# Reordered stage behind an RWKV-7 recurrence, early operand splits, and layer norms whose variance is summed with tokens on partitions

## The chip, the core and the metric

The kernel runs on one core of one Trainium2 chip. Engines as the profile names them: PE is the TensorE matmul and PEld its weight load, DVE is VectorE, ACT is ScalarE, POOL is GpSimd, SP is the queue that issues most DMAs. The metric is device microseconds (us) of one launch; lower is better.

## The reference, cut to what matters

Two identical layers work on a residual stream of 1024 tokens by 1024 features. In each, one input projection feeds three head groups: sparse attention (o_a), an RWKV-7 recurrence (o_b) and a pooling mixer (o_c). The change touches what follows the recurrence, and every layer norm (five: one on the input, two in each layer).

```
# behind the recurrence: group norm of y over heads of 64, bonus, gate
ym = y.mean(-1, keepdims=True)
yv = jnp.square(y - ym).mean(-1, keepdims=True)
yn = ((y - ym) * lax.rsqrt(yv + GN_EPS)).reshape(B, S, RWKV_WIDTH) * lnx_g + lnx_b
bonus = (jnp.sum(r_h * k_h * r_k, -1, keepdims=True) * v_h).reshape(B, S, RWKV_WIDTH)
o_b = ((yn + bonus) * g)
mix = jnp.concatenate([rms_norm(o_a, attn_norm_g), o_b, o_c], axis=-1) @ w_out
x = layer_norm(ALPHA * x + mix, ln1_g, ln1_b)
ffn = jnp.square(jax.nn.relu(x @ mlp_w1)) @ mlp_w2
ple = jax.nn.sigmoid(x @ pe_gate + pe_gate_b) * (p @ pe_proj)
x = layer_norm(ALPHA * x + ffn + ple, ln2_g, ln2_b)
```

## The kernel before

Features lie on partitions and tokens along the free dimension, in eight feature tiles (`kt`, `mt`) and two token halves of 512 (`hf`). Each engine has its own program, written out by hand in order, and the engines wait for each other by semaphores; no scheduler changes the order. A layer is a long attention stage, eight tiles of the recurrence in a loop, the stage behind the recurrence, the output projection, layer norm 1, the gate projection with the embedding, eight MLP blocks in a loop, and layer norm 2. `meet` makes four engines wait for one another, since memory is reused across it.

**Dense products.** Output projection, gate and MLP multiply operands split into a high and a low part: three matmuls for each feature tile (L1087 to L1089), so 24 for one unit (one output tile, one token half). For the output projection, ScalarE copies the eight mixed tiles into `MH` (L1389), VectorE writes what is left over into `ML` (L1993), and the weights are split the same way into `WH` (ScalarE, L1385) and `WL` (GpSimd, L1590). All of it starts behind the meeting.

**The stage behind the recurrence** works on `LP`, three feature tiles with two heads each. TensorE sums each head (mean, L1069), VectorE centres (L1948), ScalarE squares into `G1` (the profile's `SH`, L1358) and scales r (`G3`, which is `KK`, L1359), GpSimd multiplies by k (L1582), TensorE sums the bonus (L1069) and the squares (L969: tokens become partitions, the moving operand has two columns), ScalarE takes the root (L1363), VectorE inverts (L1982), TensorE spreads the inverse over each head (L978), VectorE normalises (L1960), ScalarE applies gain and offset (L1368), VectorE adds the bonus (L1966) and multiplies by the gate (L1970). `post_seq` gives TensorE's order, and a step's PSUM bank is free once the step four places earlier was read. VectorE also scales the attention's output `A3` here (L1811).

**A layer norm.** TensorE spreads the mean over all partitions (L624), VectorE subtracts it (L1613), the squares come from ScalarE for half 0 (L1131) and from GpSimd for half 1 (L1433), two buffers each. TensorE sums the squares with a matrix of 1/1024, which gives the variance on all 128 partitions for 512 tokens (L629, 128x512). ScalarE takes the root (L1134), VectorE inverts it (L1620, 128x512) and multiplies (L1628 in layer norm 1, L1624 elsewhere). Then, for layer norm 1, VectorE applies gain and offset (L1631), ScalarE makes `XH` (L1141), VectorE `XL` (L1636); elsewhere ScalarE writes `X` (L1144). In the first layer norm VectorE computes an angle and ScalarE two sines in between. The finished `X` is stored by one DMA (L609).

Of the kernel before, what the change touches and what calls it, by code (L numbers as in the profile page):

```python
# [26 lines left out]
P = 128  # L27
# [17 lines left out]
FT = DFF // FB // P  # L45
ALPHA = (2 * DEPTH) ** 0.25
# [159 lines left out]
def trunk(nc, xT, pT, pos, w_in, w_uq, w_lr, w_pool, w_out, w_gate, w_pe, w_1, w_2, par, emb, con1, con2, out):  # L206
    cs_dram = nc.dram_tensor("cs_scratch", (2, P, S), F32, kind="Internal").ap()
    with ExitStack() as ctx:
# [107 lines left out]
        G1 = SH12[:, :, :]  # L316
        G4 = sb("G4", [P, 3, S], post)
# [7 lines left out]
        Y = sb("Y", [P, KT, S], m)  # L325
        WH = sb("WH", [P, 2, KT, P], m, F32R)
# [41 lines left out]
        LN_SUMS = 2 + 2 * FB  # L368
        ln_mu, ln_xc, ln_sq, ln_sqf, ln_var, ln_std, ln_xn, ln_out = (
# [93 lines left out]
        def feats(h):  # L463
# [3 lines left out]
        post_seq = [("mean", 0), ("mean", 1), ("mean", 2), ("bonus", 0), ("var", 0), ("bonus", 1), ("bonus", 2),  # L467
                    ("spread", 0), ("spread", 1), ("gate", 0), ("spread", 2), ("gate", 1), ("gate", 2)]
        by_vector = [("mean", 0), ("mean", 1), ("mean", 2), ("bonus", 0), ("bonus", 1), ("bonus", 2), ("spread", 0),
                     ("spread", 1), ("gate", 0), ("spread", 2), ("gate", 1), ("gate", 2)]  # L470
# [28 lines left out]
        m_high, m_low = sem("m_high"), sem("m_low")  # L499
        N_SPLIT = N_WOUT + KT + FB * N_F  # L500
# [42 lines left out]
        def _(e):  # L543
# [64 lines left out]
            e.wait_ge(ln_out, 16 * (1 + 2 * DEPTH))  # L608
            e.dma_start(out, X[:, :, :]).then_inc(out_stored, 16)  # L609
            e.wait_ge(out_stored, 16)  # L610
# [3 lines left out]
        def _(e):  # L614
            def layer_norm(u, landed=None, sums=None, total=None):

                for hf in range(2):
                    if landed:
                        e.wait_ge(landed[hf], 16)
                        for kt in range(KT):  # L620
                            mm = e.matmul(BK_[4 + hf], mean_ones, Y[:, kt, hs(hf)], start=kt == 0, stop=kt == KT - 1)
                    else:
                        e.wait_ge(ln_sum, sums + (hf + 1))
                        mm = e.matmul(BK_[4 + hf], mean_ones, total[:, hf, :], start=True, stop=True)  # L624
                    mm.then_inc(ln_mu, 1)
                for hf in range(2):
                    for kt in range(KT):
                        e.wait_ge((ln_sq, ln_sq_later)[hf], u * KT + (kt + 1))
                        e.matmul(BK_[6 + hf], mean_ones, SQ[:, 2 * hf + kt % 2, :], start=kt == 0, stop=kt == KT - 1)\  # L629
                         .then_inc(ln_sqf, 1)  # L630
# [341 lines left out]

            def head_spread(bank, values, i, hf):

                for t in range(NB // 2):
                    for g in range(2):
                        w = values[:, hf, i, t, g:g + 1].broadcast_to([P, HD])
                        mm = e.matmul(bank[HD * g:HD * (g + 1), t * P:(t + 1) * P], w, ident, start=True, stop=True)  # L978
                return mm

            with e.Fori(0, DEPTH) as L:
# [72 lines left out]
                for n, (what, i) in enumerate(post_seq):  # L1054
                    for hf in range(2):
                        if n >= 4:
                            post_read(e, L, post_seq[n - 4], hf)
                        if what == "var":
                            e.wait_ge(y_sq, L * 6 + (2 * (NP - 1) + hf + 1))
                            mm = head_sums(post_bank((what, i), hf), G1, hf)  # L1060
# [10 lines left out]
                post_read(e, L, ("gate", 0), 0)  # L1071
# [3 lines left out]
                def dense(n, i, ws, high, low, kts=KT, f=0, ready=None, halves=(0, 1)):  # L1075


                    e.wait_ge(w_low, L * N_SPLIT + f * N_F + (split_seq(i) + 1))
                    s = split_seq(i) % 2
                    for hf in halves:  # L1080
                        b = 2 * (n % 2) + hf
                        e.wait_ge(d_free[b], L * D_USES + f * (N_DENSE // 2) + (n // 2 + 1))
                        for kt in range(kts):
                            if ready:
                                ready(kt, hf)
                            w, q = ws(kt), hs(hf)
                            e.matmul(BK_[b], WH[:, s, w, :], high[:, kt, q], start=kt == 0, stop=False)  # L1087
                            e.matmul(BK_[b], WH[:, s, w, :], low[:, kt, q], start=False, stop=False)  # L1088
                            mm = e.matmul(BK_[b], WL[:, s, w, :], high[:, kt, q], start=False, stop=kt == kts - 1)  # L1089
                        mm.then_inc(d_full[b], 1)  # L1090

                for mt in range(KT):
                    dense(mt, ZW + mt, lambda kt: kt, MH, ML,
                          ready=(lambda kt, hf: e.wait_ge(m_low, L * KT + (kt + 1)) if hf == 0 else None)
                          if mt == 0 else None)
# [5 lines left out]
                for mt, hf in [(0, 0), (1, 0), (0, 1), (1, 1)] + [(mt, hf) for mt in range(2, KT) for hf in range(2)]:  # L1101
                    b = 2 * (mt % 2) + hf
                    if mt < 2:
                        e.wait_ge(ln_std, (L * 2 + 2) * 2)
# [19 lines left out]
        def _(e):  # L1124
            def layer_norm(u, gain=None, offset=None, dst=None, high=None, between=None):
# [6 lines left out]
                for hf in range(2):  # L1132
                    e.wait_ge(ln_sqf, u * 16 + KT * (hf + 1))
                    e.activation(STD[:, hf, :], BK_[6 + hf], ACT.Sqrt, bias=LN_EPS).then_inc(ln_std, 1)  # L1134
                if between:
                    between()
                for n in range(2 * KT):
# [96 lines left out]
            with e.Fori(0, DEPTH) as L:  # L1234
# [120 lines left out]
                for i in range(NP):  # L1355
                    for hf in range(2):
                        post_read(e, L, ("mean", i), hf)
                        e.activation(G1[:, i, hs(hf)], LP[:, i, hs(hf)], ACT.Square).then_inc(y_sq, 1)  # L1358
                    e.activation(G3[:, i, :], BZ[:, BR + i, :], ACT.Copy, scale=par_col("rk", i))\  # L1359
                     .then_inc(bonus_half, 1)  # L1360
                for hf in range(2):
                    post_written(e, L, ("var", 0), hf)
                    e.activation(G2[:, hf, :, :, :].rearrange("p i t g -> p (i t g)"),  # L1363
                                 post_bank(("var", 0), hf)[:, 0:3 * NB], ACT.Sqrt, bias=GN_EPS, scale=1.0 / HD)\
                     .then_inc(post_scalar, 1)
                for i in range(NP):
                    e.wait_ge(y_scaled, L * 3 + (i + 1))
                    e.activation(LP[:, i, :], LP[:, i, :], ACT.Identity, bias=par_col("lb", i),  # L1368
                                 scale=par_col("lg", i)).then_inc(y_affine, 1)
                meet(e, L, 2)  # L1370

# [14 lines left out]

                split_high(L, ZW)
                for kt in range(KT):
                    e.activation(MH[:, kt, :], mixed[kt], ACT.Copy).then_inc(m_high, 1)  # L1389
# [33 lines left out]
        def _(e):  # L1423
            def layer_norm(u):

                for kt in range(KT):
# [112 lines left out]
            with e.Fori(0, DEPTH) as L:  # L1539
# [39 lines left out]
                for i in range(NP):  # L1579
                    e.wait_ge(bonus_half, L * 3 + (i + 1))  # L1580
                    settle(e)
                    e.tensor_tensor(G3[:, i, :], G3[:, i, :], BZ[:, BK + i, :], ALU.mult).then_inc(bonus_in, 1)  # L1582
                meet(e, L, 2)

# [9 lines left out]
                for i in range(ZW, MLP0 - GAP):  # L1594
# [11 lines left out]
        def _(e):  # L1606
            def layer_norm(u, between=None, affine=None, high_before=0):
# [7 lines left out]
                if between:  # L1615
                    between()
                for hf in range(2):
                    q = hs(hf)
                    e.wait_ge(ln_std, u * 2 + (hf + 1))
                    e.reciprocal(RST[:, hf, :], STD[:, hf, :])  # L1620
                    e.drain()
                    if not affine:
                        for kt in range(KT):
                            e.tensor_tensor(Y[:, kt, q], Y[:, kt, q], RST[:, hf, :], ALU.mult).then_inc(ln_xn, 1)  # L1624
                    else:
                        for n in range(KT + 3):
                            if n < KT:
                                e.tensor_tensor(Y[:, n, q], Y[:, n, q], RST[:, hf, :], ALU.mult).then_inc(ln_xn, 1)  # L1628
# [173 lines left out]
            def inverse_rms(L):  # L1802
# [3 lines left out]
                e.reciprocal(RSD[:, :], RSD[:, :])  # L1806

            def scale_attention():

                for p in range(3):  # L1810
                    e.scalar_tensor_tensor(A3[:, p, :], A3[:, p, :], par_col("ag", p), RSD[:, :], ALU.mult, ALU.mult)  # L1811
# [23 lines left out]
            def rwkv_tile(T, more):  # L1835
# [28 lines left out]
            with e.Fori(0, DEPTH) as L:  # L1864
# [76 lines left out]
                with e.Fori(0, NB - 1) as t:  # L1941
                    rwkv_tile(L * NB + t, True)
                rwkv_tile(L * NB + (NB - 1), False)
# [28 lines left out]

                for i in range(NP):
# [17 lines left out]
                for kt in range(KT):  # L1991
                    e.wait_ge(m_high, L * KT + (kt + 1))
                    e.tensor_tensor(ML[:, kt, :], mixed[kt], MH[:, kt, :].bitcast(F32), ALU.subtract)\  # L1993
                     .then_inc(m_low, 1)
# [141 lines left out]
```

## Time and profile before

| | |
|---|---|
| time, median of 3 runs | 3576.71 us (3575.73 to 3585.78) |
| the profiled execution's own time | 3576.34 us |
| its span | 3574.3 us |
| PE, PEld, DVE busy | 3274.0, 2373.5, 1913.2 us |
| ACT, POOL busy | 1053.9, 1146.4 us |
| mean granted TensorE clock | 0.965 of full |

Busy time is counted as soon as an engine has an instruction in work. An fp32 matmul appears as two rows. The chain that ended last is followed back from the last instruction; the granted clock is the share of 2.4 GHz that TensorE was given in a stretch, 1.00 or 0.50 or a mix. Times within a layer are given for the first one; the second repeats them some 1751 us later.

### The profile page before, as it was taken

What the parts mean: (1) busy time and instruction counts of PE and PEld (TensorE: products, weight loads), DVE (VectorE), ACT (ScalarE), POOL (GpSimd) and SP (SyncE); (2) the same over time, 40 slices, a digit from 0 to 9 for tenths busy, and PEclk for the clock granted to TensorE, in tenths of its full rate; (3) what the DMA queues carried; (4) which work ended last, traced back from release to release, by engine and by line L of the source; (5) the groups of instructions that cost most, each with busy time, mean ns of one, the idle gap of its engine ahead of it and who ended that gap; (6) DMA issues with size and microseconds to landing.
All of it is one profiled execution on the core that took longest, in us unless ns stands there. A gap on an engine that the chain in (4) does not pass through costs nothing.

```text
span 3574.3 us, 61403 instructions
## 1 busy us (share of the span) xinstructions
PE 3274.0 (92%) x23080; PEld 2373.5 (66%) x23080; DVE 1913.2 (54%) x3061; ACT 1053.9 (29%) x1857; POOL 1146.4 (32%) x952
## 2 busy tenths in 40 slices
PE   7989967999999999999989998689899999999997
PEld 3444435876577888888735444368675788888884
DVE  5788996444623333333467899854526133333335
ACT  3333334442212211211235343344402111221212
POOL 1175632641212222222114755155222122222221
PEclk9999979999999999999999899799999999999998
DMA  3110000001111111111111001000011111111111
GB/s 123 45 33 21 29 23 6 0 1 36 48 36 48 47 47 47 53 47 48 40 55 33 28 24 33 11 6 0 7 31 58 42 51 49 47 47 47 48 46 47
DMA packets 43861, 132.72 MB, mean 37 GB/s; under 512 B 9280, under 2 KB 11840, under 8 KB 43072
## 3 DMA queue, kind: packets, MB, share of 16 engines
q1 hardware_dynamic: 37280, 122.41, 10.5%
q10 hardware_dynamic: 6432, 8.40, 0.9%
q8 instruction: 84, 1.38, 0.2%
q14 instruction: 65, 0.53, 0.0%
HBM read 117.15 MB, written 5.24 MB: 34 GB/s over the span
## 4 chain that ended last, share of the span: by engine, by line
PE 59%; DVE 14%; issue 10%; DVEq 10%; POOLq 2%; ACT 1%; POOL 1%; DMA 1%; PEldq 0%; ACTq 0%; SPq 0%; PEld 0%
DVE M L1715 8%; DVEq L1719 8%; PE wide L1087 7%; PE bank L1089 7%; PE bank L1087 7%; PE bank L1088 7%; PE wide L1089 7%; PE wide L1088 7%; PE wide L799 3%; DVE PB L1735 2%; PE wide L629 2%; PE bank L799 2%; POOLq L1591 1%; DVE WK L1717 1%; DVEq L1716 1%
## 5 line engine op out<-in xcount | busy, mean ns | idle before, releaser
L1590 POOL TENSOR_TENSOR WL<-WR,WH 128x1024 fp32r<-128x1024 f32 x160 | 403.1, 2519 | 1479.2 <-ACT WH L1385 1478.5
L669 PE MATMUL wide<-X,WR 128*128 128x512 f32 (+1 forms) x1088 | 504.7, 608 | 11.6 <-ACT X L1144 9.4
L1385 ACT ACTIVATE WH<-WR 128x1024 fp32r<-128x1024 f32 x160 | 168.2, 1053 | 735.6 <-PE bank L1089 430.2
L2019 DVE TENSOR_TENSOR RB<-RB 128x512 f32<-128x512 f32 x128 | 88.5, 692 | 549.0 <-ACT RB L1411 549.0
L669 PEld LDWEIGHTS wide<-X,WR 128*128 128x128 f32 x1088 | 202.7, 196 | 246.9 <-issue 220.9
L1715 DVE MAX8 M<-WK 128x8 f32<-128x512 f32 (+5 forms) x342 | 314.9, 921 | 23.7
L1717 DVE MATCH_REPLACE8 WK<-M,WK 128x512 f32<-128x512 f32 (+5 forms) x342 | 309.5, 905 | 1.2 <-issue 1.2
L1087 PE MATMUL wide<-XH,WH 128*128 128x512 f32 x640 | 261.6, 409 | 18.1 <-POOLq L1591 9.5
L1087 PE MATMUL bank<-XH,WH 128*128 128x512 f32 x640 | 255.7, 400 | 0.0
L1089 PE MATMUL wide<-XH,WL 128*128 128x512 f32 x640 | 252.8, 395 | 0.0
L1088 PE MATMUL wide<-XL,WH 128*128 128x512 f32 x640 | 252.5, 395 | 0.0
L1089 PE MATMUL bank<-XH,WL 128*128 128x512 f32 x640 | 249.2, 389 | 0.0
L1088 PE MATMUL bank<-XL,WH 128*128 128x512 f32 x640 | 249.0, 389 | 0.0
L1087 PE MATMUL wide<-HH,WH 128*128 128x512 f32 x512 | 201.3, 393 | 0.0
L1088 PE MATMUL wide<-HL,WH 128*128 128x512 f32 x512 | 199.4, 389 | 0.0
L1089 PE MATMUL wide<-HH,WL 128*128 128x512 f32 x512 | 199.4, 389 | 0.0
L1089 PE MATMUL bank<-HH,WL 128*128 128x512 f32 x512 | 199.2, 389 | 0.0
L1088 PE MATMUL bank<-HL,WH 128*128 128x512 f32 x512 | 199.2, 389 | 0.0
L1087 PE MATMUL bank<-HH,WH 128*128 128x512 f32 x512 | 199.2, 389 | 0.0
L2032 DVE TENSOR_TENSOR Y<-Y,bank 128x512 f32<-128x512 f32 x128 | 87.9, 687 | 171.1 <-PE bank L1089 171.1
L799 PE MATMUL wide<-SH 64*64 64x64 f32 x3840 | 153.2, 220 | 21.2 <-POOL SH L1525 14.6
L2032 DVE TENSOR_TENSOR Y<-Y,wide 128x512 f32<-128x512 f32 x128 | 88.0, 687 | 153.7 <-PE wide L1089 153.7
(318 smaller groups left out, 6399.2 us busy)
## 6 DMA issues: line engine op xcount, KB each, us to landing
WR<-in_w SPq DMA_DIRECT2D x128, 512.0 KB, 3.5
WR<-in_w_in SPq DMA_DIRECT2D x34, 512.0 KB, 3.5
WR<-in_w_out SPq DMA_DIRECT2D x16, 512.0 KB, 3.5
WR<-in_w_gate SPq DMA_DIRECT2D x16, 512.0 KB, 5.5
Y<-in_xT SPq DMA_DIRECT2D x2, 2048.0 KB, 13.3
out_T<-X SPq DMA_DIRECT2D x1, 4096.0 KB, 11.1
QZS<-QZ ACTq DMA_DIRECT2D x48, 64.0 KB, 2.0
QZS<-QZ ACTq DMA_DIRECT2D x64, 48.0 KB, 1.9
```

The lines of the kernel that those rows point to most:

```text
L669: mm = e.matmul(BK_[hf][:, 0:q.stop - q.start], WR[:, i % RING, kt, :], X[:, kt, q], start=kt == 0, stop=kt == KT - 1)
L799: mm = e.matmul(BK_[bank][chunk(c), j * CH:(j + 1) * CH], lhs[chunk(c), 2 * j + g, :], rhs[chunk(c), 2 * j + g, :], start=True, stop=True)
L1087: e.matmul(BK_[b], WH[:, s, w, :], high[:, kt, q], start=kt == 0, stop=False)
L1088: e.matmul(BK_[b], WH[:, s, w, :], low[:, kt, q], start=False, stop=False)
L1089: mm = e.matmul(BK_[b], WL[:, s, w, :], high[:, kt, q], start=False, stop=kt == kts - 1)
L1385: e.activation(WH[:, split_seq(i) % 2, :, :], WR[:, i % RING, :, :], ACT.Copy).then_inc(w_high, 1)
L1590: e.tensor_tensor(WL[:, s, :, :], WR[:, i % RING, :, :], WH[:, s, :, :].bitcast(F32), ALU.subtract)
L1715: e.max(M8[:, :], src)
L1717: e.match_replace(work, M8[:, :], src, DROPPED if drop else BIG)
L1719: e.drain()
L2019: e.tensor_tensor(RB[:, b, :], RB[:, b, :], RB[:, b, :], ALU.mult).then_inc(square_ready, 1)
L2032: e.tensor_tensor(Y[:, i, hs(hf)], Y[:, i, hs(hf)], BK_[b], ALU.add).then_inc(d_free[b], 1)
```

## The change

It has four parts.

1. Behind the recurrence, the squares are summed as each becomes ready, and the variance stands in front of the bonuses. Two of the eight operand tiles are split (high and low) and two more copied high, and the first weight block is split high and low, all ahead of the meeting; the first unit of the output projection takes the tiles in the order 6, 0, 1, 2, 3, 4, 5, 7. Paddings and the map `LOW_AT` place these operands where nothing live is overwritten.
2. The attention's output is scaled in the recurrence's loop, 128 tokens a tile.
3. A layer norm sums its squares with tokens on partitions: 4 matmuls with two moving columns for each tile instead of one with 512. Root and inverse are then taken of 128x8, and the inverse is spread back by 4 transposing matmuls per half (`spread_inverse`); VectorE multiplies straight from PSUM. GpSimd keeps four of its eight squares, ScalarE takes the others. In layer norm 2, ScalarE writes three tiles of X ahead of the second root.
4. The output is stored in four quarters as they are finished.

```diff
@@ sync @@
-            e.wait_ge(ln_out, 16 * (1 + 2 * DEPTH))
-            e.dma_start(out, X[:, :, :]).then_inc(out_stored, 16)
+            for n in range(KT // 2, 2 * KT + 1, KT // 2):
+                k, q = slice((n - 1) % KT // (KT // 2) * (KT // 2), (n - 1) % KT + 1), hs((n - 1) // KT)
+                e.wait_ge(ln_out, 16 * 2 * DEPTH + n)
+                e.dma_start(out[:, k, q], X[:, k, q]).then_inc(out_stored, 16)
@@ tensor: layer norm @@
-                        e.matmul(BK_[6 + hf], mean_ones, SQ[:, 2 * hf + kt % 2, :], start=kt == 0, stop=kt == KT - 1)\
-                         .then_inc(ln_sqf, 1)
+                        for t in range(LN_TOK):
+                            mm = e.matmul(BK_[6 + hf][:, 2 * t:2 * t + 2], SQ[:, 2 * hf + kt % 2, t * P:(t + 1) * P],
+                                          mean_ones[:, 0:2], start=kt + t == 0, stop=kt + t == KT + LN_TOK - 2)
+                        mm.then_inc(ln_sqf, 1)
+                        if (hf, kt) in ((1, 1), (1, KT - 1)):
+                            spread_inverse(u, int(kt > 1))
+            def spread_inverse(u, hf):
+                e.wait_ge(ln_inv, u * 2 + (hf + 1))
+                for t in range(LN_TOK):
+                    mm = e.matmul(BK_[6 + hf][:, t * P:(t + 1) * P],
+                                  STD[:, hf, 2 * t:2 * t + 1].broadcast_to([P, P]), ident, start=True, stop=True)
+                mm.then_inc(ln_spread, 1)
@@ tensor: behind the recurrence @@
-                post_read(e, L, ("gate", 0), 0)
+                post_read(e, L, ("spread", 2), 0)
                 keep_clock(2, 4)
                 meet(e, L, 2)
@@ scalar: layer norm @@
+                ahead = 3 if high is None and not between else 0
+                later_square(1)
+                deviation(0)
+                for kt in range(3, KT, 2):
+                    later_square(kt)
+                for n in range(ahead):
+                    write_out(n)
+                deviation(1)
+                if between:
+                    between()
+                for n in range(ahead, 2 * KT):
+                    write_out(n)
@@ scalar: behind the recurrence @@
+                split_mixed(L, 0, 2)
                 split_high(L, ZW)
                 ...
+                split_mixed(L, 2, M_EARLY)
                 ...
                 meet(e, L, 2)
+                split_mixed(L, M_EARLY, KT)
@@ gpsimd @@
-                for kt in range(KT):
+                for kt in range(0, KT, 2):
                 ...
+                split_low(ZW)
                 meet(e, L, 2)
@@ vector: layer norm @@
-                    e.reciprocal(RST[:, hf, :], STD[:, hf, :])
+                def invert(hf):
+                    e.wait_ge(ln_std, u * 2 + (hf + 1))
+                    e.reciprocal(STD[:, hf, 0:2 * LN_TOK], STD[:, hf, 0:2 * LN_TOK]).then_inc(ln_inv, 1)
                 ...
-                            e.tensor_tensor(Y[:, kt, q], Y[:, kt, q], RST[:, hf, :], ALU.mult).then_inc(ln_xn, 1)
+                            e.tensor_tensor(Y[:, kt, q], Y[:, kt, q], BK_[6 + hf], ALU.mult).then_inc(ln_xn, 1)
+                            if (hf, kt) == (0, KT - 3):
+                                invert(1)
@@ vector: recurrence and behind @@
+                scale_attention(t)
                 ...
-                bonus(0)
-                scale_attention()
-                for i in range(1, NP):
-                    bonus(i)
+                lows(0, M_AHEAD)
                 for hf in range(2):
                     post_read(e, L, ("var", 0), hf)
                 e.reciprocal(g2, g2).then_inc(y_rstd, 1)
+                bonus(0)
                 normalise(0)
                 normalise(1)
+                bonus(1)
                 gated(0)
                 normalise(2)
+                bonus(2)
                 gated(1)
                 gated(2)
                 meet(e, L, 2)
-                for kt in range(KT):
+                lows(M_AHEAD, KT)
```

VectorE behind the recurrence, before: `G` is the bonus, `A` the attention's output, and the RECIPROCAL the inverse of the root.

```order
L1954 TENSOR_TENSOR G<-wide,BZ 128x512
L1811 SCALAR_TENSOR_TENSOR A<-A,PAR,RSD 128x1024 x3
L482 REGISTER_ALU
L1954 TENSOR_TENSOR G<-bank,BZ 128x512
L482 REGISTER_ALU
L1954 TENSOR_TENSOR G<-bank,BZ 128x512
L482 REGISTER_ALU
L1954 TENSOR_TENSOR G<-wide,BZ 128x512
L482 REGISTER_ALU
L1954 TENSOR_TENSOR G<-wide,BZ 128x512
L487 REGISTER_ALU
L1982 RECIPROCAL G<-G 128x48
```

The same engine and place now, from the last centring on.

```order
L2033 SCALAR_TENSOR_TENSOR LP<-wide,LP 128x512
L2063 TENSOR_TENSOR ML<-PZ,MH 128x1024
L2063 TENSOR_TENSOR ML<-A,MH 128x1024
L495 REGISTER_ALU
L2072 RECIPROCAL G<-G 128x48
L490 REGISTER_ALU
L2039 TENSOR_TENSOR G<-wide,BZ 128x512
L490 REGISTER_ALU
L2039 TENSOR_TENSOR G<-wide,BZ 128x512
L490 REGISTER_ALU
L2045 TENSOR_TENSOR LP<-LP,bank 128x512
```

All bonuses have moved behind the inverse, the attention's scaling has left this place, and two low parts stand in front of the inverse.

ScalarE at the same place, before: `KK` is r scaled, `G` the root, `LP` gain and offset.

```order
L1359 ACTIVATE KK<-BZ,PAR 128x1024
L482 ISA
L1363 ACT_TABLE_LOAD
L1363 ACTIVATE G<-wide 128x24
L482 REGISTER_ALU
L1363 ACTIVATE G<-wide 128x24
L1367 ISA
L1368 ACTIVATE LP<-LP,PAR 128x1024
```

And now: `MH` is the high part of an operand tile, `WH` that of the weights.

```order
L1446 ACTIVATE KK<-BZ,PAR 128x1024 x2
L1439 ACTIVATE MH<-PZ 128x1024
L1438 ISA
L1439 ACTIVATE MH<-A 128x1024
L1420 ISA
L1431 ACTIVATE WH<-WR 128x1024
L490 ISA
L1452 ACT_TABLE_LOAD
L1452 ACTIVATE G<-wide 128x24
```

Three copies that stood behind the meeting stand in front of the root here; two more follow it.

TensorE in the first layer norm, before: the mean, then the sums of squares.

```order
L613 UNCONDITIONAL_BRANCH
L621 MATMUL wide<-Y,C 128x512 x16
L629 MATMUL wide<-SQ,C 128x512 x16
L981 UNCONDITIONAL_BRANCH
L981 ISA
```

Now (`STD` is the inverse root, spread by the identity in `C`).

```order
L624 UNCONDITIONAL_BRANCH
L632 MATMUL wide<-Y,C 128x512 x16
L646 MATMUL wide<-C,SQ 128x2 x40
L656 MATMUL wide<-C,STD 128x128 x4
L646 MATMUL wide<-C,SQ 128x2 x24
L656 MATMUL wide<-C,STD 128x128 x4
L1023 UNCONDITIONAL_BRANCH
```

Each of the 16 wide matmuls has become four narrow ones, and two groups of spreads stand among them: the first behind the second tile of half 1, the other at the end, ahead of the projection that follows.

## Rows read from the trace of the kernel before

**Rows 1.** Stretches: each engine's busy time (instructions), granted clock, DMA share, GB/s.

```profile
794.00:835.00 41.00, 33.54 (x188) 20.37 (x186) 27.76 (x32) 16.27 (x20) 9.34 (x4) 0.90 0.00 1
928.00:980.00 52.00, 44.73 (x121) 22.36 (x120) 48.90 (x69) 19.00 (x29) 11.68 (x9) 0.93 0.21 81
980.00:1780.00 800.00, 795.27 (x3439) 645.78 (x3437) 275.27 (x399) 155.12 (x213) 176.14 (x70) 1.00 0.14 46
```

**Rows 2.** The chain behind the recurrence: start, us, engine and line.

```profile
802.41 6.55 PE wide L969 x48
...
839.61 5.67 DVE ML L1993 x3
```

**Rows 3.** ScalarE behind the recurrence: start, us, instruction, idle before and releaser.

```profile
800.86 1.13 ACT L1359 ACTIVATE KK<-BZ,PAR 128x1024 f32<-128x1024 f32 x1
...
809.00 0.19 ACT L1363 ACTIVATE G<-wide 128x24 f32<-128x24 f32 x1 [3.79 <-PE wide L969]
...
830.58 1.06 ACT L1385 ACTIVATE WH<-WR 128x1024 fp32r<-128x1024 f32 x1 [4.96 <-PEq L522]
831.54 2.93 ACT L1389 ACTIVATE MH<-A 128x1024 fp32r<-128x1024 f32 x3
```

**Rows 4.** VectorE behind the recurrence, in order of time.

```profile
803.06 5.43 DVE L1811 SCALAR_TENSOR_TENSOR A<-A,PAR,RSD 128x1024 f32<-128x1024 f32 x3
...
815.18 0.44 DVE L1982 RECIPROCAL G<-G 128x48 f32<-128x48 f32 x1
816.90 0.69 DVE L1960 TENSOR_TENSOR LP<-LP,wide 128x512 f32<-128x512 f32 x1 [1.28 <-PE wide L978]
...
828.47 1.29 DVE L1970 TENSOR_TENSOR BZ<-wide,LP 128x512 f32<-128x512 f32 x2 [0.15 <-issue]
```

**Rows 5.** One line: ns min/median/max of a low part.

```profile
L1993 DVE TENSOR_TENSOR ML<-A,MH x6: 1210/1213/2535, 832.6 to 2587.1; 128x1024 fp32r<-128x1024 f32 x6
```

**Rows 6.** VectorE in a tile of the recurrence.

```profile
670.36 0.62 DVE L1847 TENSOR_TENSOR MT<-wide,MT 128x192 f32<-128x192 f32 x2 [4.80 <-PE wide L873]
```

**Rows 7.** Two stretches of 1 us within L969's two-column matmuls.

```profile
805.00:806.00 1.00, 1.00 (x11) 1.00 (x11) 1.00 (x1) 0.19 (x1) 0.01 (x1) 1.00 0.00 0
806.00:807.00 1.00, 1.00 (x7) 1.00 (x7) 1.00 (x2) 0.00 (x0) 0.00 (x0) 0.55 0.00 0
```

**Rows 8.** TensorE, 128 moving columns, 128-column weights: start, us.

```profile
1813.74 3.73 PE L656 MATMUL wide<-X,WR 128*128 128x128 f32 x32
```

**Rows 9.** Layer norm 1 of the first layer, in order of time, all engines.

```profile
948.18 0.60 ACT L1134 ACTIVATE STD<-wide 128x512 f32<-128x512 f32 x1 [9.11 <-PE wide L629]
...
959.59 0.69 DVE L1636 TENSOR_TENSOR XL<-Y,XH 128x512 fp32r<-128x512 f32 x1
960.37 3.35 DVE L1620 RECIPROCAL RST<-STD 128x512 f32<-128x512 f32 x1
...
977.60 1.48 DVE L1636 TENSOR_TENSOR XL<-Y,XH 128x512 fp32r<-128x512 f32 x2 [0.16 <-ACT XH L1141]
...
979.93 1.88 PE L1107 MATMUL wide<-PE_IN,PEW 128*128 128x512 f32 x4
```

**Rows 10.** Layer norm 2 of the first layer: TensorE's and ScalarE's first work behind it.

```profile
1803.98 9.92 PE L669 MATMUL wide<-X,WR 128*128 128x512 f32 x16 [4.07 <-ACT X L1144]
...
1816.30 1.28 ACT L1257 ACT_TABLE_LOAD   x1 [4.48 <-issue]
```

**Rows 11.** The first layer norm: VectorE's first inverse, ScalarE's second root.

```profile
44.08 3.35 DVE L1620 RECIPROCAL RST<-STD 128x512 f32<-128x512 f32 x1 [0.16 <-issue]
...
48.82 0.60 ACT L1134 ACTIVATE STD<-wide 128x512 f32<-128x512 f32 x1 [11.25 <-PE wide L629]
```

**Rows 12.** The last layer norm's writes, then DMA issues: KB each, median us to landing.

```profile
3551.44 11.38 ACT L1144 ACTIVATE X<-Y,PAR 128x512 f32<-128x512 f32 x16
...
out_T<-X SPq DMA_DIRECT2D x1, 4096.0 KB, 11.1
WR<-in_w SPq DMA_DIRECT2D x128, 512.0 KB, 3.5
```

More of the change, by code:

```diff
@@ L368, in trunk @@
         LN_SUMS = 2 + 2 * FB
+        ln_inv, ln_spread = sem("ln_inv"), sem("ln_spread")
+        LN_TOK = HALF // P
+        SQ_ACT = [kt % 2 for kt in range(KT)]
         ln_mu, ln_xc, ln_sq, ln_sqf, ln_var, ln_std, ln_xn, ln_out = (
@@ L464, in feats @@
             return slice(HD * (h % 2), HD * (h % 2) + HD)
[L467 to L470, printed above, removed]
+        post_seq = [("mean", 0), ("mean", 1), ("mean", 2), ("var", 0), ("bonus", 0), ("spread", 0), ("spread", 1),
+                    ("bonus", 1), ("gate", 0), ("spread", 2), ("bonus", 2), ("gate", 1), ("gate", 2)]
+        by_vector = [use for use in post_seq if use[0] != "var"]
         by_scalar = [("var", 0)]
@@ L971, in head_sums, with variances @@
                 return mm
+            def variances(L):
+                for i in range(NP):
+                    for hf in range(2):
+                        e.wait_ge(y_sq, L * 6 + (2 * i + hf + 1))
+                        bank = post_bank(("var", 0), hf)
+                        for t in range(NB // 2):
+                            c, q = (i * (NB // 2) + t) * 2, hf * HALF + t * P
+                            mm = e.matmul(bank[:, c:c + 2], G1[:, i, q:q + P], block_ones[:, 0:P:HD],
+                                          start=True, stop=True)
+                        if i == NP - 1 and hf == 0:
+                            mm.then_inc(post_full, 1)
+                return mm
             def head_spread(bank, values, i, hf):
@@ L1070, in _, with dense @@
                         mm.then_inc(post_full, 1)
-                post_read(e, L, ("gate", 0), 0)
+                post_read(e, L, ("spread", 2), 0)
                 keep_clock(2, 4)
                 meet(e, L, 2)
-                def dense(n, i, ws, high, low, kts=KT, f=0, ready=None, halves=(0, 1)):
+                def dense(n, i, ws, high, low, kts=KT, f=0, ready=None, halves=(0, 1), order=range(KT), low_at=range(KT)):
                     e.wait_ge(w_low, L * N_SPLIT + f * N_F + (split_seq(i) + 1))
@@ L1082, in dense @@
                         e.wait_ge(d_free[b], L * D_USES + f * (N_DENSE // 2) + (n // 2 + 1))
-                        for kt in range(kts):
+                        for k, kt in enumerate(order[:kts]):
                             if ready:
-                                ready(kt, hf)
+                                ready(k, hf)
                             w, q = ws(kt), hs(hf)
-                            e.matmul(BK_[b], WH[:, s, w, :], high[:, kt, q], start=kt == 0, stop=False)
-                            e.matmul(BK_[b], WH[:, s, w, :], low[:, kt, q], start=False, stop=False)
-                            mm = e.matmul(BK_[b], WL[:, s, w, :], high[:, kt, q], start=False, stop=kt == kts - 1)
+                            e.matmul(BK_[b], WH[:, s, w, :], high[:, kt, q], start=k == 0, stop=False)
+                            e.matmul(BK_[b], WH[:, s, w, :], low[:, low_at[kt], q], start=False, stop=False)
+                            mm = e.matmul(BK_[b], WL[:, s, w, :], high[:, kt, q], start=False, stop=k == kts - 1)
                         mm.then_inc(d_full[b], 1)
@@ L1131, in layer_norm, with later_square, deviation, write_out @@
                     e.activation(SQ[:, kt % 2, :], Y[:, kt, hs(0)], ACT.Square).then_inc(ln_sq, 1)
-                for hf in range(2):
+                def later_square(kt):
+                    e.wait_ge(ln_xc, u * 16 + (KT + kt + 1))
+                    if kt >= 2:
+                        e.wait_ge(ln_sqf, u * 16 + (KT + kt - 1))
+                    e.activation(SQ[:, 2 + kt % 2, :], Y[:, kt, hs(1)], ACT.Square).then_inc(ln_sq, 1)
+                def deviation(hf):
                     e.wait_ge(ln_sqf, u * 16 + KT * (hf + 1))
[L1134 to L1137, printed above, removed]
+                    e.activation(STD[:, hf, 0:2 * LN_TOK], BK_[6 + hf][:, 0:2 * LN_TOK], ACT.Sqrt, bias=LN_EPS)\
+                     .then_inc(ln_std, 1)
+                def write_out(n):
                     hf, kt = n // KT, n % KT
@@ L1592, in split_low @@
                     e.drain().then_inc(w_used, 1 + GAP * (i == MLP0 - GAP - 1))
-                for i in range(ZW, MLP0 - GAP):
+                for i in range(NP):
+                    e.wait_ge(bonus_half, L * 3 + (i + 1))
+                    settle(e)
+                    e.tensor_tensor(G3[:, i, :], G3[:, i, :], BZ[:, BK + i, :], ALU.mult).then_inc(bonus_in, 1)
+                split_low(ZW)
+                meet(e, L, 2)
+                for i in range(ZW + 1, MLP0 - GAP):
                     split_low(i)
```

103 lines of the change are left out of this document (62 added, 41 removed).

## The prediction

> **What bounds the kernel now.** I read the page first: TensorE is busy for 92% of the span. The stretches then say where it is not the bound. From 980 to 1780 (gate projection and MLP blocks) it works all the time at the full clock: 3439 rows in 795.27 us, 0.231 us a row, so 24 matmuls of one unit take 5.5 us [rows 1]. The change doesn't touch that. The two stretches it touches are behind the recurrence (794 to 835) and in layer norm 1 (928 to 980), where TensorE is busy too but with waits between, and its clock is granted at 0.90 and 0.93 [rows 1]. So I read the chain there, then VectorE's and ScalarE's own rows. Behind the recurrence the chain goes through the sums of squares (6.55 us) and ends in the low parts of the operand tiles [rows 2]. ScalarE has its second root only at 809.00, and VectorE inverts at 815.18 and ends at 828.47 + 1.29 = 829.76 [rows 3, 4]. In layer norm 1 VectorE is the bound: two inverses of 3.35 us, then products, gain and low parts up to 979.1, and the gate's fourth unit starts at 979.93 [rows 9].
>
> **Behind the recurrence, up to the meeting.** The squares are now summed as they come, between TensorE's other work, so the variance waits for ScalarE alone. ScalarE ends its old work at 801.99 [rows 3]. Before its roots now stand two high copies (2.93/3 = 0.98 each), the weight's (1.06), a table load (1.28, rows 10) and the roots (0.19 each): 801.99 + 1.95 + 1.06 + 1.28 + 0.4 = 806.7. VectorE inverts at about 807.0, 8.2 us earlier than at 815.18. Its two early low parts (1.21 each, rows 5) lie in the gap before. Its scaling of the attention, 5.43 us at 803.06, leaves, but that lay beside the waits for squares and bonus and gives nothing by itself [rows 4]. From the inverse to the end it took 829.76 - 815.18 = 14.6 us. Now three bonuses follow it too, each a pair of 1.29 us, some 1.5 with waits [rows 4]; the first fills the 1.28 us in which VectorE waited for the first spread [rows 4]. So 807.0 + 14.6 + 4.5 - 1.3 = 824.8. TensorE has had no work for some 4 us before the spreads, which are new in the path between the bonuses; if its clock is then at half, they and the gate matmuls cost VectorE between 0 and 3.3 us. I take 1.8: 826.6, against 829.8, a gain of 3 us (1.5 to 5).
>
> **From the meeting to the first unit.** ScalarE's first work behind the meeting starts at 830.58 [rows 3], and the last low part ends at 839.61 + 5.67 = 845.3 [rows 2], 14.7 us later; TensorE follows VectorE tile by tile. Now weights, two low parts and four high parts are there already. Six low parts are left. The first three at 1.21 us [rows 5]; the last three at 1.89 us, as in rows 2 (5.67 for three), since GpSimd's next weight split still falls beside them: 3.6 + 5.7 = 9.3 us, with a start 9.5. That is 5.2 us gained (3.5 to 6.5). Together 8.2 us a layer, 16.4 for two (10 to 22).
>
> **The recurrence.** Each tile gets three scalings of 128x128 on VectorE, with an address computed. They stand ahead of an addition for which VectorE idles 4.80 us [rows 6]. A whole 128x1024 scaling took 5.43/3 = 1.81 us [rows 4], so a slice costs at most that, and the three together at most 5.4, at least an eighth, 0.7. I take 0.9, hidden. Were the idle time gone, 16 tiles would cost 14 us.
>
> **A sum of squares.** A feature tile takes 8 rows of two columns instead of two rows of 512. The rows to go by are L969's, same form: 11 rows in a microsecond at full clock, 7 in the next, in which the clock falls to 0.55 on average [rows 7]. So a tile takes 0.73 us or 1.14 us, against about 0.9 for two wide rows (1.88 us for four, rows 9). In this trace TensorE's row was busy for 1.00 of both stretches, its weight loads too, and the clock fell nevertheless. I take the fall to come in the layer norms as well, and so 1.14 from the middle of half 0 on. A spread is 8 rows of 128 columns: L656 takes 3.73/32 = 0.117 us a row [rows 8], 0.9 us, and up to 1.9 at half clock.
> The Trainium skill, "TensorE: Matmul & The Clock Gate", Part 1, says that the low level is the default and that activity of TensorE releases it. Taken so that a TensorE that always has an instruction in work stays up, its clock would hold through the narrow sums; rows 7 show that it did not. By that reading the sum is rival B's, by the row it is mine.
>
> **Layer norm 1, twice.** Half 0 ends as before (about 938.4). Then two sums (2.3), the first spread (1.7): VectorE's first product near 942.6, no later or earlier than before. Six more sums of half 1, with squares shared by ScalarE and GpSimd, last until 949.8; the second root falls at 950.0, against 948.18 [rows 9]. High parts wait for it on ScalarE, VectorE's low parts for them: +1.9. But the second inverse of 3.35 us at 960.37 is gone [rows 9], so the last low part moves from 977.60 + 1.48 = 979.1 to 977.6. TensorE now waits too: the spread of half 1 needs the second inverse, which stands behind VectorE's sixth product, and that behind two low parts. It starts the embedding near 956 instead of 949, then has three units of 1.8 + 5.5 = 7.3 us, the first partly at half clock: 956.4 + 21.9 + 1.4 = 979.7, against 979.93. So nothing to gain: -0.2 each. With a full clock throughout, the root falls at 947.9 and the fourth unit at 976.5: -3.4. The other end is +3.
>
> **Layer norm 2 of the first layer.** TensorE used to wait 4.07 us and start its 9.92 us unit at 1803.98; ScalarE took 4.48 us and a table load until 1817.6, later than the unit's end at 1813.9 [rows 10]. Now the last spread ends near 1804.0 and the unit starts 4.07 later: 1808.1 + 9.9 = 1818.0. +0.3 (-1.7 to +2). Here TensorE's sequence takes over from ScalarE's.
>
> **The first layer norm.** VectorE computes an angle until 44.08 [rows 11]. TensorE now stands before the first spread until VectorE has inverted behind it, with six sums of half 1 queued; the second root comes near 51 instead of 48.82 [rows 11], and sines and writes of X behind it. A narrow root gives back 0.4. +1.8 (0 to +3.5).
>
> **The last layer norm and the output.** As in layer norm 2 without a successor: three writes of 11.38/16 = 0.71 us [rows 12] go ahead of the second root, no 3.35 us inverse stands before half 1. ScalarE's writes set the end: -1.0 (-2.5 to +0.5). The output was one DMA of 4096 KB, 11.1 us; 512 KB take 3.5 [rows 12]. Between them 1024 KB take 3.5 + 512 x 7.6/3584 = 4.6 us. Pieces come every 4 x 0.71 = 2.8 us, and 1024 KB more cost 2.2, so they don't queue: -6.5 (-4 to -7.6).
>
> **Sum.** -16.4 - 0.4 + 0.3 + 1.8 - 1.0 - 6.5 = -22.2 us. From the profiled execution's own 3576.3 that gives 3554.1; the median shown is 0.4 above it: 3554.5.
>
> **Rivals.**
> - A, this forecast: 3550 to 3561, chance 0.50.
> - B, the clock stays full through the narrow sums. Then -3.4 twice in layer norm 1, -1.7, +0.8 and -2.5 in the others, and no 1.8 behind the recurrence: -16.4 - 3.6 - 6.8 - 1.7 + 0.8 - 2.5 - 6.5 = -36.7, 3540. For it: squares pause between and so do the wide matmuls of before, which kept the clock. Against it: rows 7. 0.12.
> - C, a new wait takes the place of the removed one in the layer norms: root, inverse and spread are now three engines in turn, twice in each. At 2.5 us more in each of five, 3554.5 + 12.5 = 3567. For it: TensorE's place for the spread is fixed, so any lateness stops the sums behind it. Against it: the inverse shrinks from 3.35 us to little. 0.22.
> - D, the meeting comes no earlier: with bonus and spread alternating, TensorE's matmuls, not VectorE, set the path. 3554.5 + 6 = 3560.5. For it: 14.6 us of VectorE's work had TensorE's work done ahead. 0.12.
> - E, slower: TensorE stays at half clock behind layer norm 1 through the first three gate units. These are 21.9 us at full and take twice that, so 3554.5 + 2 x 20.5 = 3595.5. It is slower than before from 11.1 us a layer more than I counted. Against it: the mean of 0.93 over 52 us [rows 1] is 7 us at half, so the clock came back by itself in this place. 0.04.
>
> Measurements of this kernel can tell about 0.3% (10.7 us) from no change. A, B and D are faster by more, C in half of it: 0.85 faster, 0.11 within, 0.04 slower. The range 3542 to 3568 leaves out most of B below, part of C and E above.
>
> **What would show it.** Right: VectorE's 128x48 inverse some 8 us earlier than before, counted from the last centring; the last low part some 8 us earlier; narrow sums at 7 rows a microsecond; layer norm 1's fourth unit within 1 us of its place; the first layer norm later by 2; from the last write of X to the span's end under 5 us. Wrong: an idle VectorE before its additions in the recurrence gone; the second root of layer norm 1 over 3 us later; the granted clock of the first gate units at half for over 10 us; VectorE waiting for spreads or gates behind the recurrence.

## The result and the profile after

| | kernel before | changed kernel |
|---|---|---|
| time, median | 3579.45 us | 3640.55 us (3639.28 to 3644.71) |
| ratio to before | | 1.0171, 95% interval 1.0152 to 1.0189 |
| span of the profiled execution | 3574.3 us | 3637.5 us |
| mean granted clock | 0.965 | 0.950 |

The forecast was 3554.5 us, faster; the kernel is 1.7% slower. To see where, I put the same instruction of both traces side by side at the start of every stage. The table gives how much longer (+) or shorter each stage is than before; its sum is 3637.5 - 3574.3 = 63.2 us. The first norm ends with the first write of X, layer norm 1 with the first gate unit that ScalarE reads out of PSUM, layer norm 2 together with the attention behind it at the recurrence's first tile, and the last norm with the end of the last write of X. The recurrence's eighth tile is counted to the stage behind it, which ends with VectorE's first residual (its first addition of X to the output projection).

| stage | changed | forecast | e4 | e5 | e9 |
|---|---|---|---|---|---|
| first layer norm | +5.4 | +1.8 | +5.3 | -0.9 | +2.9 |
| attention of layer 0 | +3.8 | 0 | +2.8 | +0.4 | +1.1 |
| recurrence, 7 tiles, two layers | -0.3 | 0 | +0.3 | +0.5 | -0.6 |
| behind the recurrence, two | -16.9 | -16.4 | -17.3 | -16.6 | -15.6 |
| output projection, two | +5.3 | 0 | +3.0 | +1.6 | +2.6 |
| layer norm 1, two | +9.3 | -0.4 | +11.6 | 0.0 | -8.1 |
| gate and MLP, two | +45.9 | 0 | +3.3 | +1.0 | +2.1 |
| layer norm 2 and attention of layer 1 | +9.5 | +0.3 | +7.1 | 0.0 | +1.0 |
| last layer norm | +7.3 | -1.0 | +5.8 | 0.0 | -2.8 |
| output | -6.0 | -6.5 | -6.9 | -6.9 | -6.9 |

(e4, e5 and e9 are experiments below.) Two stages make the result: the MLP, in which the change edits nothing, and the layer norms.

**The MLP.** One row of [rows 1] is this stretch before. Here are 100 us of it, first before, then after (the columns are those of rows 1, for TensorE alone; x counts the matmul rows that overlap the stretch):

```profile
1100.00:1200.00 100.00, 100.00 (x441) 1.00 0.15 48
```

```profile
1100.00:1200.00 100.00, 100.00 (x430) 1.00 0.14 43
```

TensorE is busy all the time and at the full clock in both, but does 11 rows fewer. The timeline shows that it is every row that is longer, not some wait between them, before:

```profile
1100.05 0.39 PE L1089 MATMUL bank<-XH,WL 128*128 128x512 f32 x1
1100.28 0.39 PE L1087 MATMUL bank<-XH,WH 128*128 128x512 f32 x1
1100.50 0.39 PE L1088 MATMUL bank<-XL,WH 128*128 128x512 f32 x1
1100.73 0.39 PE L1089 MATMUL bank<-XH,WL 128*128 128x512 f32 x1
```

and after:

```profile
1100.16 0.40 PE L1132 MATMUL wide<-XH,WL 128*128 128x512 f32 x1
1100.40 0.39 PE L1130 MATMUL wide<-XH,WH 128*128 128x512 f32 x1
1100.63 0.40 PE L1131 MATMUL wide<-XL,WH 128*128 128x512 f32 x1
1100.86 0.39 PE L1132 MATMUL wide<-XH,WL 128*128 128x512 f32 x1
```

Three rows are 0.68 us apart before, 0.70 after. 100/441 and 100/430 give 0.2267 and 0.2326 us a row. A layer has 72 weight splits x 48 rows = 3456 such rows in gate and MLP: 3456 x 0.006 = 21 us, of the 23 measured (45.9 for two layers).

**Layer norm 1.** Before, TensorE summed the first ten feature tiles in 9.42 us, 0.94 a tile:

```profile
930.73 9.42 PE L629 MATMUL wide<-SQ,C 128*128 128x512 f32 x20
```

The rows that answer to it, and to [rows 9], are now:

```profile
934.12 13.87 PE L646 MATMUL wide<-C,SQ 128*128 128x2 f32 x80
947.85 2.05 PE L656 MATMUL wide<-C,STD 128*128 128x128 f32 x8
949.69 10.24 PE L646 MATMUL wide<-C,SQ 128*128 128x2 f32 x48
964.17 1.65 PE L656 MATMUL wide<-C,STD 128*128 128x128 f32 x6 [4.24 <-DVE STD L1693]
```

48 narrow rows, six feature tiles, take 10.24 us: 0.213 a row, 1.71 a tile. TensorE goes through all sums without a stop and sets the pace; ScalarE waits for it before the second root, which is 28.6 us behind the last residual (931.33), against 20.2 before:

```profile
959.97 0.18 ACT L1184 ACTIVATE STD<-wide 128x8 f32<-128x8 f32 x1 [2.72 <-PE wide L646]
```

The granted clock fell at about 938, some 34 rows into the sums, with TensorE busy for the whole of both stretches:

```profile
938.00:940.00 2.00, 2.00 (x12) 0.51 0.97 397
940.00:950.00 10.00, 10.00 (x49) 0.50 0.33 134
```

**Behind the recurrence**, counted from the end of the last centring (799.57 before, 808.69 now), VectorE's inverse comes 7.1 us earlier and its last low part ends 8.9 us earlier (845.52 now):

```profile
813.95 3.37 DVE L2063 TENSOR_TENSOR ML<-A,MH 128x1024 fp32r<-128x1024 f32 x1
817.24 0.44 DVE L2072 RECIPROCAL G<-G 128x48 f32<-128x48 f32 x1
...
842.13 3.39 DVE L2063 TENSOR_TENSOR ML<-PZ,MH 128x1024 fp32r<-128x1024 f32 x1
847.03 0.69 DVE L2089 SCALAR_TENSOR_TENSOR Y<-X,wide 128x512 f32<-128x512 f32 x1 [1.51 <-PE wide L1132]
```

### The profile page after: what moved, and what is told of

Read it like the earlier page. It is cut to its first block, busy times and chain, and to the rows that moved or that the text cites. A ratio compares the mean times of both kernels' runs of the same rounds, so it can differ in the third digit from the quotient of the medians.

```text
span 3637.5 us, 62624 instructions
## 1 busy us (share of the span) xinstructions
PE 3369.9 (93%) x23640; PEld 2484.6 (68%) x23640; DVE 1871.3 (51%) x3103; ACT 1062.4 (29%) x1877; POOL 1125.2 (31%) x932
## 3 DMA queue, kind: packets, MB, share of 16 engines
q1 hardware_dynamic: 39248, 122.41, 10.5%
## 4 chain that ended last, share of the span: by engine, by line
PE 60%; DVE 14%; issue 10%; DVEq 10%; POOLq 2%; ACT 1%; DMA 1%; POOL 1%; ACTq 1%; PEldq 0%; SPq 0%; PEld 0%
DVE M L1796 8%; DVEq L1800 8%; PE wide L1130 7%; PE bank L1132 7%; PE bank L1130 7%; PE bank L1131 7%; PE wide L1131 7%; PE wide L1132 7%; PE wide L827 3%; PE wide L646 3%; DVE PB L1816 2%; PE bank L827 2%; POOLq L1658 1%; DVE WK L1798 1%; DVEq L1797 1%
```

## The experiments

**Where do the slower rows come from?** Part 1 of the change has two paddings, lines that do no work. One of them is `sb("under_wh", [P, W_PAD], m)`, with `W_PAD` = 819 elements. It moves WH, WL, ML and all behind them 3296 bytes up in SBUF. In the program's table of tiles WH started at 166560 bytes before and starts at 169856 now; the moving tiles XH, XL, HH and HL stay at 35488, 68256, 101024 and 117408. Divided by 256, all moving tiles leave 160, and so did WH and WL before; now these leave 128.

Experiment e1, on the kernel before:

```
+        sb("under_wh", [P, 819], m)
         WH = sb("WH", [P, 2, KT, P], m, F32R)
```

> The kernel before, in which only WH and all tiles behind it in SBUF start 3296 bytes later, as in the changed kernel: WH then starts at a multiple of 64 bytes, as before it started 32 past one; no instruction is changed. Theory 1 (the start of the tiles): TensorE's rows with WH or WL as weights start every 0.2327 us instead of 0.2267, as in the changed kernel, in about 7700 rows, and the time is 3577 + 50 = 3625 us, from 3618 to 3630. Theory 2 (the slower rows come from the changed code, the order of the contraction or the clock): rows at 0.2267 and 3577 us within 5.

Measured 3628.28 us, ratio 1.0128 (1.0107 to 1.0149), rows as in the changed kernel:

```profile
1100.00:1200.00 100.00, 100.00 (x429) 1.00 0.15 48
```

The padding alone makes them, and 42.0 us in gate and MLP with them; theory 2 is out. Experiment e2 has 827 in place of 819:

> The same with 32 bytes more, so that WH starts 32 past a multiple of 64 bytes again, but as far away as in the changed kernel. Theory 1 (only the place within 64 bytes): rows at 0.2267 us, 3577 us within 5. Rival (the distance, or the region of SBUF that the tiles now fall in): rows at 0.2327, 3625 us. Theory 2: 3577 us.

3580.85 us, ratio 1.0006 (0.9995 to 1.0016), and the rows are back:

```profile
1100.00:1200.00 100.00, 100.00 (x441) 1.00 0.15 48
```

Not the distance, but the place. Experiment e3, on the kernel before:

```
         WR = sb("WR", [P, RING, KT, P])
+        sb("under_all", [P, 8])
```

> The kernel before with every tile behind the ring of weights 32 bytes later, so that the moving tiles (XH, XL, HH, HL, MH, X) and WH, WL all start at a multiple of 64 bytes; no instruction is changed. If the place of the weights alone counts: rows at 0.2327, 3625 us. If it is that weights and moving tiles have different places within 64 bytes: rows at 0.2267, 3577 us. If the moving tiles have their own price too: rows slower than 0.2327, over 3630 us. Theory 2: 3577 us.

3577.28 us, ratio 1.0002 (0.9988 to 1.0016), 441 rows. Moved together, weights and moving tiles cost nothing: what counts is where they stand to each other. Three more, all on the kernel before: e6 has both edits with 8 elements each, e7 `under_wh` with 16 and e10 with 32.

> The kernel before with XH, XL, HH, HL, MH and X at a multiple of 64 bytes and WH, WL, ML and what stands behind them 32 past one: the two kinds of tile differ again, but the other way round than in the changed kernel. If it is the difference that costs: rows at 0.2327 us and 3577 + 50 = 3627 us. If it is weights at a multiple of 64 beside moving tiles 32 past one alone: rows at 0.2267 and 3578 us.

> The kernel before with WH and all behind it 64 bytes later: the same place within 64 bytes as the moving tiles, another within 128 and 256. If only the place within 64 bytes counts: rows at 0.2267 us, 3578 us within 5. If it is the place within 128 or more: rows at 0.2327, 3627 us.

> The kernel before with WH and all behind it 128 bytes later. So far the rows were fast (0.2267 us) where WH started 0 or 3328 bytes (13 x 256) farther from the moving tiles than before, or moved with them, and slow (0.2327) at 3296, 32 and 64 bytes. If starts must be equal within 128 bytes: fast, 3579 us within 5. If within 256 bytes: slow, 3626 us within 5.

Measured 3626.36 us (1.0128, 1.0111 to 1.0144), 3626.94 (1.0130, 1.0112 to 1.0148) and 3620.71 (1.0121, 1.0101 to 1.0140), with 429, 429 and 431 rows in the same 100 us; of e10:

```profile
1100.00:1200.00 100.00, 100.00 (x431) 1.00 0.15 48
```

So my guess of 64 bytes was too small. By how much WH's start moved against the moving tiles': 0 (before, e3) and 3328 bytes (e2, 13 x 256) are fast; 32, 64, 128 and 3296 (13 x 256 - 32) are slow, by 43 to 49 us. The runs fit a rule of 256 bytes: 128 is slow, and 3328 isn't a multiple of 512. It rests on e2 alone for a distance other than 0, and nothing between 128 and 256 was run. What in the chip makes it they don't show. The Trainium skill, "SBUF — State Buffer", section "SBUF: two separate sides", says that TensorE never waits for another engine at SBUF. By that, what is met here would lie between TensorE's own two reads; no run here shows that.

Experiment e4, on the changed kernel, moves WH up by 32 bytes and the tiles whose place it takes over along with it:

```
-G4_PAD, W_PAD = 4109, 819
+G4_PAD, W_PAD = 4109, 827
...
         KK = sb("KK", [P, 3, S], m)
+        sb("under_ka", [P, 8], m)
         KA = sb("KA", [P, 3, S], m)
```

> The changed kernel with WH, WL, ML and what stands behind them, and KA, LP and the tiles of the recurrence, 32 bytes later, so that WH starts 32 past a multiple of 64 bytes as in the kernel before. Theory 1: rows at 0.2267, the two MLP stretches 22 us shorter each and the output projections 2.6 each, 3640 - 50 = 3590 us, from 3584 to 3596. Theory 2: no change, 3640 us within 5. What is left above the kernel before, about 13 us, is then the layer norms' (30 us more) less the gains behind the recurrence (17) and at the output (6).

3590.61 us, ratio 1.0031 (1.0021 to 1.0041): 50 us less than the changed kernel. The table shows gate and MLP at +3.3 of 45.9 us.

**What makes the norms longer?** Experiment e5 is e4's kernel with the layer norms of before:

> The changed kernel with the starts of tiles of the fourth experiment and the layer norms of the kernel before (wide sums of squares, a root and an inverse of 128x512 for each half); the new order behind the recurrence, the early splits and the output in four pieces stay. Theory 3 (the narrow sums at half clock cost the norms 5.4 + 4.6 + 7.5 + 4.7 + 7.3 = some 30 us): 3590.6 - 30 = 3561, or, counted from the kernel before, 3579 - 16.8 - 6.0 = 3556: from 3553 to 3563. Rival (the norms' 30 us belong to something else that stays, such as the early weight split or the output's pieces): 3575 to 3591.

3555.49 us, ratio 0.9930 (0.9915 to 0.9945). All four stages with layer norms are back within 1 us of before, and the gains behind the recurrence and at the output are whole. Experiment e8, on e4's kernel, behind the narrow sums of a feature tile:

```
                         mm.then_inc(ln_sqf, 1)
+                        for _ in range(2):
+                            e.matmul(BK_[0], ident.bitcast(mybir.dt.bfloat16)[:, 0:P],
+                                     C1[:, 0:HALF // 2].bitcast(mybir.dt.bfloat16), start=True, stop=True)
```

> The fourth experiment's kernel in which TensorE does two more matmuls of 512 bfloat16 columns, whose result nobody reads, behind the narrow sums of every feature tile of a layer norm (160 in all, about 0.21 us each at full clock). Theory 3 (the norms lose by the clock at which the narrow sums run, 8 rows in 1.71 us at half, 0.86 at full): if the added matmuls hold the clock up, a tile takes 0.86 + 0.43 = 1.29 us instead of 1.71, layer norm 1's second root comes some 4 us earlier, and the time is 3590.6 - 5 x 4 = 3571, from 3566 to 3580. If they don't hold it, a tile takes 1.71 + 0.86 and the time is 3590.6 + 5 x 9 = 3636. Rival (the norms lose by the extra turns of root, inverse and spread, not by the sums): 3590 to 3600 at either clock.

3629.75 us, 39 more than e4. The clock fell all the same in every norm: 7.0 us behind the first sum of layer norm 1, against 2.6 in e4, and 4.2 against 4.1 in layer norm 2. Both kinds of row then ran at half of it:

```profile
954.39 1.71 PE L647 MATMUL wide<-C,SQ 128*128 128x2 f32 x8
955.96 1.01 PE L651 MATMUL wide<-C 128*128 128x512 bf16 x2
956.76 1.71 PE L647 MATMUL wide<-C,SQ 128*128 128x2 f32 x8
```

That is near the second branch of theory 3 (3636) and speaks against the rival (work added to the sums would have cost nothing), but it doesn't show the norms with the clock up. Experiment e9 does, on e4's kernel:

```
-                            mm = e.matmul(BK_[6 + hf][:, 2 * t:2 * t + 2], SQ[:, 2 * hf + kt % 2, t * P:(t + 1) * P],
-                                          mean_ones[:, 0:2], start=kt + t == 0, stop=kt + t == KT + LN_TOK - 2)
+                            mm = e.matmul(BK_[6 + hf][:, t * P:(t + 1) * P], SQ[:, 2 * hf + kt % 2, t * P:(t + 1) * P],
+                                          mean_ones, start=kt + t == 0, stop=kt + t == KT + LN_TOK - 2)
```

> The fourth experiment's kernel with one edit in the layer norms: a sum of squares has 128 moving columns of ones instead of 2 (the root reads two of every 128); the number of TensorE's rows, the roots, inverses and spreads stay. Rows of 128 columns of fp32 take 0.117 us at full clock in the projections and their clock stays up there. Theory 3 (the norms lose by the clock that falls in the sums): the clock stays up, a feature tile takes 0.94 us instead of 1.71, the second root of layer norm 1 comes 6 to 9 us earlier, and the time is 3590.6 less 5 x 6 to 5 x 8: 3550 to 3561. If the clock falls all the same: a tile takes 1.9 us, 3590 to 3600. Rival (the extra turns of root, inverse and spread): within 5 of 3590 though the clock stays up.

3552.15 us, ratio 0.9932 (0.9918 to 0.9945). The same count of rows, each with 64 times the columns, is faster, because the clock stays up in layer norm 1, layer norm 2 and the last norm:

```profile
928.76 9.66 PE L647 MATMUL wide<-C,SQ 128*128 128x128 f32 x80
938.25 1.06 PE L657 MATMUL wide<-C,STD 128*128 128x128 f32 x8
939.14 1.95 PE L647 MATMUL wide<-C,SQ 128*128 128x128 f32 x16
```

```profile
936.00:946.00 10.00, 9.20 (x78) 1.00 0.19 77
929.00:938.00 9.00, 9.00 (x78) 1.00 1.00 411
```

```profile
945.98 0.18 ACT L1185 ACTIVATE STD<-wide 128x8 f32<-128x8 f32 x1 [1.73 <-PE wide L647]
```

At the full clock, within a tile, a row of 2 columns (changed kernel, up to 938) and a row of 128 (e9) both start 0.111 us behind the one before, so the wider rows cost next to nothing. A tile takes 0.97 us instead of 1.71, the second root is now 20.0 us behind the last residual (925.97), and layer norm 1 is 4.1 us shorter than before the change: the big inverses that went are a gain at last. The Trainium skill, "TensorE: Matmul & The Clock Gate", Part 1, says that the chip sets the clock by how busy TensorE has been. Here TensorE was busy for all of 938 to 950 in the changed kernel, where the clock was at half, and for all of 929 to 938 in e9, where it stayed full. Only the columns differ, so what counts as busy can't be read from that row.

The first norm is still +2.9 in e9. Experiment e11 puts VectorE's first inverse there ahead of the third addition of its angle instead of behind the angle:

> The ninth experiment's kernel, in which VectorE inverts half 0 of the first layer norm inside its work on the angle, ahead of that work's third addition (L1753) instead of behind all of it. In the ninth TensorE waited 4.21 us there for the inverse (root 37.47, inverse 42.41, spread 42.66). Theory: the inverse comes near 38.9, the spread near 39.2, VectorE's first product near 43.0 instead of 44.78 (the angle still lies ahead of it), the second root near 49 instead of 52.17, and the first write of X 2.5 to 3.2 us earlier than at 56.16: 3552.2 - 3 = 3549. Rival (the squares of half 1 set the time there): the write of X within 1 us, 3552.

3548.13 us, ratio 0.9918 (0.9905 to 0.9930), the fastest of all. TensorE waits 0.58 us for the inverse, not 4.21, and ScalarE writes X from 51.12 instead of 56.16:

```profile
39.02 0.20 DVE L1693 RECIPROCAL STD<-STD 128x8 f32<-128x8 f32 x1
```

```profile
39.27 1.16 PE L657 MATMUL wide<-C,STD 128*128 128x128 f32 x8 [0.58 <-DVE STD L1693]
```

It gained 5.0 us there, more than I expected: TensorE, without the long wait, kept its full clock as well (1.00 from 38 to 44; in e9 0.82 from 38 to 42 and 0.50 from 42 to 45), and the spread took 1.16 us, not 2.08.

**The output alone**, e12 on the kernel before:

> The kernel before with one edit: the output goes in four DMAs of 1024 KB, each behind the fourth, eighth, twelfth and sixteenth write of X. In the changed kernel 5.5 us passed from the last write of X to the end, in the kernel before 11.5. Theory: 5.5 here too and 3578 - 6 = 3572. Rival (the pieces slow each other or ScalarE's writes): over 7 us behind the last write, or writes of X longer than 11.4 us in all, 3575 or more.

3572.49 us, ratio 0.9983 (0.9974 to 0.9992). The writes of X take 11.38 us as before and end at 3570.63, the span at 3575.2: 4.6 us behind the last write, against 11.5 before.

```profile
out_T<-X SPq DMA_DIRECT2D x4, 1024.0 KB, 4.2
```

## Why the prediction was wrong

- **"The change doesn't touch that"**, of the stretch from 980 to 1780. This sentence failed, and with it 51 of the 85 us between the forecast change (-22.2) and the profile's (+63.2): 45.9 in gate and MLP, 5.3 in the output projections. The padding was in the change, and I read it as room for tiles that now live together. It moves the weights of the very rows that fill this stretch. e1 shows the cost by itself, e4 its removal.
- **A sum of squares: the term of 1.14 us a tile.** It measured 1.71. I took 11 and 7 rows in one microsecond [rows 7] as the rates at full and half clock. But such a count holds every row that overlaps the stretch, and the second microsecond was a mixed one. In the same group of 48 rows [rows 2] the rows start 0.111 us apart up to 806.07 and 0.213 apart behind it, which is 0.89 and 1.71 a tile. With 1.71 the wide rows' 0.94 a tile [rows 9] is little more than half of the narrow ones', not about as much. For the same reason half 0 of layer norm 1 did not end as before: its root came 13.3 us behind the last residual, not 10.5. The forecast that the clock would fall was right; what it costs was mis-sized, by 0.57 us a tile and for ten to fourteen tiles a norm, most of the 31 us by which the norms missed (+31.5 against +0.7, the second attention's share within it).
- **The first norm** has the wait that I named, TensorE before the first spread until the angle is done, but in the changed kernel it was only 1.23 us, since the sums ahead of it, part of them at half clock, ended late themselves. Faster sums (e9) took 2.4 of the 5.4 us away and let the wait grow to 4.21; taking that away (e11) gave 5.0 more.

```profile
42.46 2.07 PE L656 MATMUL wide<-C,STD 128*128 128x128 f32 x8 [1.23 <-DVE STD L1693]
```

- **Behind the recurrence** the steps held (D is out: the meeting came earlier): 16.9 us gained against 16.4, VectorE's end 3.2 us earlier (forecast 3), the last low part 8.9 (8.2). The inverse gained 7.1, not 8.2, since the second early low part lay beside GpSimd's product for the bonus and took 3.37 us, not 1.21.
- **The recurrence** hid its scalings: -0.3 us in both layers together, VectorE's idle time before L1932 still 4.57 us in the last tile.
- **The output** gained 6.0 us against 6.5, and in e12 exactly the 4.6 us behind the last write that I had worked out.
- **Rivals.** E had the sign but not the cause: the clock is back at full behind layer norm 1. B's terms for a full clock in layer norm 1 (-3.4), layer norm 2 (-1.7) and the last norm (-2.5) are close to what e9 measured (-4.1, -2.8 up to the first write of X, and -2.8); in the first norm it had +0.8 against +2.9. C's new wait exists in the norms, but TensorE's sums, not the turns of three engines, are what it waits for. Of the signs that I had named for being wrong, one came: the second root of layer norm 1, 8.4 us later.

The 3.8 us in the attention of layer 0 can't be put down to the change. The same stage is 0.4 to 4.4 us longer in e4, e5, e8, e9 and e11, and in the kernel before with nothing but tiles moved it lies between -1.1 (e3) and +3.4 us (e10). Each of these is one profiled execution.

## What to carry to other kernels

Read padding and moved tiles in a diff as an edit of every instruction that reads them: look at where weights and moving operands of the hot matmuls start, and compare rows per 100 us, not the busy share, which was 100% in both. Price narrow matmuls from a stretch that is wholly at one clock, by last start less first start, and never by what a short window counts. A sum with 2 moving columns was no cheaper a row than one with 128 (0.111 us from one row to the next at the full clock), and it took the clock down. In layer norm 1 the granted clock was 0.50 from 940 to 965, 0.62 from 965 to 970, where the wide rows begin, and 1.00 from 970 to 980.

## What the runs showed that I had not expected

- Rows of 512 columns with fp32r operands start every 0.2267 us when the weights' and the moving tile's starts leave the same remainder by 256 bytes, and every 0.2326 when they don't: 2.6%, at the same granted clock and busy share. The fp32 rows of the projections (weights WR, moving X) didn't show it: in e3 their starts differ by 32 bytes more than before, and a row takes 611 ns on average against 615.
- 80 matmul rows of 128 columns took 9.66 us, and the first 80 of two columns 13.87.
- Two matmuls of 512 bfloat16 columns behind every 8 narrow rows did not hold the clock.
- A TENSOR_TENSOR of 128x1024 on VectorE took 1.22 us alone and 3.4 us beside GpSimd's product for the bonus and beside its weight split.
